# A two-layer f32 transformer kernel: the first feed-forward block in seven block products too, and modulation work cut into 1 KB slabs inside its pairs

## What is computed

```python
for l in range(DEPTH):                       # DEPTH = 2
    sh1, sc1, g1, sh2, sc2, g2, sh3, sc3, g3 = split(silu(c) @ w_mod[l] + b_mod[l], 9)
    # ... and the same nine rows from c_ctx for the context tokens
    x = x + 0.5 * g1 * swiglu(modulate(x, nw[0], sh1, sc1), ffn1_up[l], ffn1_down[l])
    # ... token mixer: w_in projection, pooling, gated linear attention, sigmoid gates, w_out
    x = x + 0.5 * g3 * swiglu(modulate(x, nw[2], sh3, sc3), ffn2_up[l], ffn2_down[l])
return rmsnorm(x, final_norm_w)
```

## Time and profile before

| what | value |
|---|---|
| median of 3 runs | 2866.95 us (2865.28 to 2867.62) |
| the profiled execution | 2867.43 us |
| its span, first to last instruction | 2865.6 us |
| instructions | 40473 |
| TensorE (PE) busy | 2824.5 us, 99% |
| PE weight loads busy | 2473.3 us, 86% |
| VectorE (DVE) busy | 1803.7 us, 63% |
| ScalarE (ACT) busy | 917.3 us, 32% |
| mean granted TensorE clock | 0.997 |
| DMA | 275.41 MB, mean 96 GB/s |

### The profile page before, as it was taken

How to read it: one execution, slowest core, us unless ns; L and a number is a source line. 1 busy time by engine, 2 the same in 40 slices (tenths; PEclk the granted TensorE clock), 3 DMA queues, 4 the chain that set the end, 5 groups by cost and what they waited for, 6 DMA issues and landing times.

```text
span 2865.6 us, 40473 instructions
## 1 busy us (share of the span) xinstructions
PE 2824.5 (99%) x15912; PEld 2473.3 (86%) x15912; DVE 1803.7 (63%) x3089; ACT 917.3 (32%) x1403; POOL 246.0 (9%) x257
## 2 busy tenths in 40 slices
PE   7999999999999999999999999999999999999998
PEld 6888888888888888899999889999988778888886
DVE  4676676657447738677766767785756667553334
ACT  4221211254332224232333523322445333432223
POOL 1000000022700011000000200000021600200000
PEclk9999999999999999999999999999999999999999
DMA  7344444322124424324122342232223144333332
GB/s 241 101 132 121 120 122 130 98 74 52 30 72 128 118 64 123 91 67 117 54 81 69 91 119 61 81 97 73 71 54 98 41 121 144 111 110 96 95 96 81
DMA packets 462077, 275.41 MB, mean 96 GB/s; under 512 B 15914, under 2 KB 460116, under 8 KB 461908
## 3 DMA queue, kind: packets, MB, share of 16 engines
q1 hardware_dynamic: 459700, 269.09, 33.0%
q10 hardware_dynamic: 2208, 4.00, 0.4%
HBM read 270.95 MB, written 2.10 MB: 95 GB/s over the span
## 4 chain that ended last, share of the span: by engine, by line
PE 93%; DVE 3%; ACT 2%; issue 1%; DMA 1%; SPq 0%; POOL 0%; ACTq 0%; POOLq 0%; DVEq 0%
PE ps L1609 44%; PE ps L1623 22%; PE ps L1862 11%; PE ps L1869 5%; PE ps L1830 2%; PE ps L1655 2%; PE ps L1835 1%; PE ps L974 1%; PE ps L954 1%; DVE wlo L2262 1%; ACT whi L1960 0%; DMA wraw<-in_ffn_up 0%; ACT hhi L2025 0%; PE ps L942 0%; DVE hlo L2366 0%
## 5 line engine op out<-in xcount | busy, mean ns | idle before, releaser
L1609 PE MATMUL ps<-hhi,whi 128*128 128x512 f32 x2112 | 625.6, 357 | 1.4 <-ACT whi L1960 1.4
L1609 PE MATMUL ps<-hlo,whi 128*128 128x512 f32 x2112 | 617.5, 353 | 0.0
L2262 DVE TENSOR_TENSOR wlo<-wraw,whi 128x1024 fp32r<-128x1024 f32 (+2 forms) x331 | 363.1, 1100 | 331.1 <-ACT whi L1960 328.7
L1960 ACT ACTIVATE whi<-wraw 128x1024 fp32r<-128x1024 f32 (+2 forms) x323 | 310.9, 963 | 721.3 <-PE ps L1623 615.2
L1623 PE MATMUL ps<-hhi,wlo 128*128 128x512 f32 x2112 | 437.2, 355 | 0.0
L1609 PEld LDWEIGHTS ps<-hhi,whi 128*128 128x128 f32 x2112 | 344.2, 189 | 61.1 <-issue 3.6
L1623 PEld LDWEIGHTS ps<-hhi,wlo 128*128 128x128 f32 x2112 | 342.4, 188 | 58.5 <-issue 3.2
L1609 PEld LDWEIGHTS ps<-hlo,whi 128*128 128x128 f32 x2112 | 343.8, 188 | 56.6 <-issue 0.5
L2281 DVE SCALAR_TENSOR_TENSOR macc<-modraw,cond,macc 128x256 f32<-128x256 f32 x588 | 240.9, 481 | 0.0
L1609 PE MATMUL ps<-mhi,whi 128*128 128x512 f32 x576 | 176.8, 359 | 0.0
L1609 PE MATMUL ps<-mlo,whi 128*128 128x512 f32 x576 | 176.1, 358 | 0.0
(11 more groups left out here) (299 smaller groups left out, 4702.5 us busy)
## 6 DMA issues: line engine op xcount, KB each, us to landing
wraw<-in_ffn_up SPq DMA_DIRECT2D x176, 512.0 KB, 4.8
modraw<-in_w_mod SPq DMA_DIRECT2D x84, 512.0 KB, 3.6
wraw<-in_w_in SPq DMA_DIRECT2D x64, 512.0 KB, 4.0
wraw<-in_ffn_down SPq DMA_DIRECT2D x64, 384.0 KB, 4.1
wraw<-in_ffn_down SPq DMA_DIRECT2D x32, 512.0 KB, 4.1
wraw<-in_w_mod SPq DMA_DIRECT2D x64, 256.0 KB, 3.1
first_mod<-in_w_mod SPq DMA_DIRECT2D x8, 1024.0 KB, 12.1
wraw<-in_w_out SPq DMA_DIRECT2D x16, 512.0 KB, 3.7
```

What stands on the lines that cost most here:

```text
L1609: nc.tensor.matmul(o, whi[:, slot, k, :], a[:, k * NT + t0:k * NT + t0 + n], start=(k == 0 and a is hi), stop=False)
L1960: nc.scalar.activation(whi[:, slot2, k, n], wraw[:, slot4, k, n], ACT.Copy).then_inc(hi_split, 1)
L2262: ins = nc.vector.tensor_tensor(wlo[:, slot2, k, n], wraw[:, slot4, k, n], whi[:, slot2, k, n].bitcast(F32), ALU.subtract)
```

## The change

Block (0,0) becomes a block with fast groups, in the four groups of the others. The modulation jobs that it hosted have to go elsewhere, and for that there is a *flow*: in every block with fast groups five jobs are cut into 40 slabs of one chunk (128 partitions of 1 KB). Fast pairs take two slabs each, one ahead of the sum at L2556 (slot 0) and one ahead of that at L2561 (slot 1); the `down` phase of the four-chunk group takes 3, 3, 3 and 0. So the slabs are 0 to 11 in the first fast group, 12 to 19 in the second, 20 to 28 in the down phase, 29 to 39 in the last, and slabs 7, 15, 23, 31 and 39 end a job with the transpose and the reduction. The ring for the loads has three places, and the transposed copy (`turned_flow`) lies over two of them. So the load of a job's first two slabs waits for the reduction of the job before. Each phase in which a flow job ends forms a batch of its own. Besides, the `down` phase that makes the token sums hosts one job, the gates loop of layer 0 one more (11), and the first group of (1,1) four instead of two. `mtmp_fast` has one buffer instead of two, `stmp_fast` half a buffer, the early silu waits for `late_m`, and the transposed copy of a job in a fast block's `down` phase lies over its second slab, whose load now waits for the reduction.

```diff
-FAST = {(0, 1): 1, (1, 0): 1}
-FFN_JOBS = {(0, 0): (6, 4, 8, 4, 6, 0), (0, 1): (6, 0, 0, 3, 0, 0, 0, 0), (1, 0): (6, 0, 0, 3, 0, 0, 0, 0),
-            (1, 1): (2, 0, 0, 0, 0, 0)}
-GATES_SPOTS = ([(i, place) for i in range(1, DC) for place in ((0, 1, 2) if i < DC - 1 else (0, 1))],
+FAST = {(0, 0): 1, (0, 1): 1, (1, 0): 1}
+FFN_JOBS = {(0, 0): (4, 1, 0, 3, 0, 0, 0, 0), (0, 1): (6, 1, 0, 3, 0, 0, 0, 0), (1, 0): (6, 1, 0, 3, 0, 0, 0, 0),
+            (1, 1): (4, 0, 0, 0, 0, 0)}
+FLOW_JOBS = 5
+RING = 3
+GATES_SPOTS = ([(0, 2), *((i, place) for i in range(1, DC) for place in (0, 1, 2))],
...
             add("up", layer, n, ffn, t, jobs[2 * t], parts=parts, lead=2 if t == 0 and (layer, ffn) in ((0, 0), (1, 1)) else 0,
-                fast=t >= FAST.get((layer, ffn), len(groups)))
+                fast=t >= FAST.get((layer, ffn), len(groups)),
+                flow=(2,) * n if t >= FAST.get((layer, ffn), len(groups)) else ())
             add("down", layer, DC // 2, ffn, t, jobs[2 * t + 1], parts=parts,
+                flow=(3, 3, 3, 0) if (layer, ffn) in FAST and n < DC // 2 + 1 else (),
...
+    turned_flow = lay("turned_flow", [P, 4 * P])
...
-    stmp_fast = lay("stmp_fast", [P, NT])
-    lay("pad_trows", [P, P])
+    stmp_fast = lay("stmp_fast", [P, HALF])
+    flow_first = lay("flow_first", [P, 2, 2 * P])
...
-    mtmp_fast = lay("mtmp_fast", [P, 2, NT])
+    mtmp_fast = lay("mtmp_fast", [P, NT])
...
-                elif ph["kind"] == "gates" and s == 1:
+                elif (ph["kind"] == "gates" or ph["kind"] == "down" and is_fast(ph)) and s == 1:
                     sp.wait_ge(mod_reduced, j)
...
+            def load_flow(ph, n):
+                for f in ph["flow"][n] if ph["flow"] else ():
+                    job, k = flow_number[f // DC], f % DC
+                    layer = (job >= MODJ) * 1
+                    if f == ph["flow"][0][0]:
+                        sp.wait_ge(mod_reduced, ph["seq"])
+                    if f >= RING:
+                        sp.wait_ge(flow_step, 2 * (f - RING + 1))
+                    if k < 2 and f >= DC:
+                        sp.wait_ge(flow_reduced, f // DC)
+                    sp.dma_start(ring_at(f), wm[layer][:, k, (job - layer * MODJ) * 2 * P:(job - layer * MODJ + 1) * 2 * P]
+                                 ).then_inc(flow_loaded[f % RING], 16)
...
+                            if isinstance(i, int):
+                                load_flow(ph, 2 * i + h)
...
                 for j in fast_pairs(ph):
                     for s in range(2):
                         load_unit(u0 + 2 * j + s, (u0 + 2 * j + s) % 4,
                                   up[:, :, s * D_FF + (f0 + j) * P:s * D_FF + (f0 + j + 1) * P], DC)
+                    load_flow(ph, j)
...
+            def flow(ph, n, which):
+                for f in [*ph["flow"][n]][which] if ph["flow"] else ():
+                    k = f % DC
+                    dve.wait_ge(flow_loaded[f % RING], 16 * (f // RING + 1))
+                    for c in range(2):
+                        if k == 0:
+                            ins = nc.vector.tensor_scalar(macc_flow[:, c, :], ring_at(f), cond[:, c * DC:c * DC + 1],
+                                                          None, ALU.mult)
+                        else:
+                            dve.wait_ge(flow_step, 2 * f - 1 + c)
+                            ins = nc.vector.scalar_tensor_tensor(
+                                out=macc_flow[:, c, :], in0=ring_at(f), scalar=cond[:, c * DC + k:c * DC + k + 1],
+                                in1=macc_flow[:, c, :], op0=ALU.mult, op1=ALU.add)
+                        ins.then_inc(flow_step, 1)
+                    if k == DC - 1:
+                        dve.wait_ge(flow_step, 2 * (f + 1))
+                        nc.vector.transpose(turned_flow[:], macc_flow[:].rearrange("p c n -> p (c n)")
+                                            ).then_inc(flow_turned, 1)
+                        dve.wait_ge(flow_turned, f // DC + 1)
+                        nc.vector.tensor_reduce(mred_flow[:, f // DC % FLOW_JOBS], turned_flow[:].rearrange("p (j n) -> p j n", n=BLK),
+                                                mybir.AxisListType.X, ALU.add).then_inc(flow_reduced, 1)
...
                         m_early(j - 1)
                         fast_lo_term(ph, j, 4)
                         m_lo(j - 1)
+                    flow(ph, j, slice(0, 1))
                     dve.wait_ge(term_done, done + 2)
                     dve.wait_ge(first_kept, q + 1)
                     steps.link(nc.vector.tensor_tensor(u2[:], fast_bank(p, 1), u2[:], ALU.add))
                     if j == 0 and jobs_pending(ph):
                         mod_finish(jobs_pending(ph))
                     fast_lo_term(ph, j, 5 if j else 4)
+                    flow(ph, j, slice(1, 2))
                     dve.wait_ge(term_done, done + 3)
                     nc.vector.tensor_tensor(late, fast_bank(p, 2), u2[:], ALU.add).then_inc(fifth_read, 1)
...
```

More of the change, by code:

```diff
@@ L104, in make_plan, with add @@
 def make_plan():
-    plan, unit, pair, job, fast_pairs = [], 0, 0, START_JOBS, 0
-    def add(kind, layer, pairs, ffn=0, third=0, jobs=0, units=None, parts=BOTH, ahead=None, fast=False, lead=0):
-        nonlocal unit, pair, job, fast_pairs
+    plan, unit, pair, job, fast_pairs, seq, flowed, numbers = [], 0, 0, START_JOBS, 0, 0, 0, []
+    def add(kind, layer, pairs, ffn=0, third=0, jobs=0, units=None, parts=BOTH, ahead=None, fast=False, lead=0, flow=()):
+        nonlocal unit, pair, job, fast_pairs, seq, flowed
+        slabs, first = [], flowed
+        for n in flow:
+            n = min(n, DC * FLOW_JOBS * ([*FAST].index((layer, ffn)) + 1) - flowed)
+            slabs.append(range(flowed, flowed + n))
+            flowed += n
+        done = range(first // DC, flowed // DC)
         units = 2 * pairs if units is None else units
         plan.append(dict(kind=kind, layer=layer, ffn=ffn, third=third, unit=unit, pair=pair, parts=parts, ahead=ahead,
-                         pairs=pairs, units=units, job=job - lead, lead=lead, jobs=jobs, fast=fast, first_fast=fast_pairs))
-        unit, pair, job = unit + units, pair + pairs, job + jobs
+                         pairs=pairs, units=units, job=job - lead, lead=lead, jobs=jobs, seq=seq, flow=slabs, done=done, fast=fast, first_fast=fast_pairs))
+        unit, pair, job, seq = unit + units, pair + pairs, job + jobs, seq + jobs
+        plan[-1]["turn"] = job
+        numbers.extend(range(job, job + len(done)))
+        job += len(done)
         fast_pairs += pairs if fast else 0
@@ L138, in make_plan @@
     assert job == DEPTH * MODJ
[L139 removed]
+    return plan, numbers
 def proj_pairs():
@@ L428, in build @@
     mod_reduced = sem("mod_reduced")
+    flow_loaded = [sem(f"flow_loaded{i}") for i in range(RING)]
+    flow_step = sem("flow_step")
+    flow_turned = sem("flow_turned")
+    flow_reduced = sem("flow_reduced")
     mod_done = sem("mod_done")
@@ L609, in jobs_of, with seq_of, ring_at @@
     def jobs_of(ph):
-        n0 = ph["job"] + ph["lead"]
-        return n0, n0 + ph["jobs"]
+        n0 = ph["job"] + ph["lead"] if ph["jobs"] else ph["turn"]
+        return n0, n0 + (ph["jobs"] or len(ph["done"]))
+    def seq_of(ph, job):
+        return job - ph["job"] - ph["lead"] + ph["seq"]
+    def ring_at(f):
+        return (flow_first[:, 0], flow_first[:, 1], flow_last[:])[f % RING]
     def halves_at(ph, i, h, place, jobs):
@@ L621, in halves_at @@
             return ((ph["job"] + q // 2, q % 2),)
+        if makes_t(ph):
+            return ((ph["job"], i),) if ph["jobs"] and h == 0 and place else ()
         hosted = 2 * i + h < ph["jobs"] if ph["kind"] == "down" and is_fast(ph) else jobs
@@ L641, in slab_count @@
         each = slabs(ph) // 2
-        return 16 * each * job + 16 * (before - each * jobs_of(ph)[0] + s // 2 + 1)
+        return 16 * each * (job - ph["job"] - ph["lead"]) + 16 * (before + s // 2 + 1)
     def mod_work(ph):
@@ L656, in mred_of @@
     def mred_of(ph):
+        if ph["kind"] == "down" and is_fast(ph):
+            return mred_down, 0
         return (mred_gates, 0) if ph["kind"] == "gates" else (mred, plan.index(ph) % 2)
     def jobs_before(ph):
-        return min(ph["job"] + ph["jobs"], DEPTH * MODJ)
+        return min(ph["turn"], DEPTH * MODJ)
     def m_base(l, ffn, third=0):
@@ L804, in jobs_pending @@
         before = plan[plan.index(ph) - 1] if ph is not plan[0] else ph
-        return before if before["jobs"] and ph is not plan[0] else None
+        return before if (before["jobs"] or before["done"]) and ph is not plan[0] else None
     def batches_before(ph):
-        return sum(1 for p in plan[:plan.index(ph)] if p["jobs"])
+        return sum(1 for p in plan[:plan.index(ph)] if p["jobs"] or p["done"])
     def peeled(ph, a):
@@ L2267, in mod_add @@
             def mod_add(ph, job, half):
-                n, per = job - START_JOBS, DC // slabs(ph)
```

(3 more changed lines are left out.)

90 lines of the change are left out of this document (58 added, 32 removed).

## The result

The changed kernel takes **2894.94 us** (median of 4 runs, 2893.39 to 2897.51) against 2867.28 for the kernel before beside it: ratio 1.0098, 95% interval 1.0086 to 1.011. It is slower by 28 us. The forecast was 2879.5 us, and the time lies 2 us above the upper end of the range, 2893. The profiled execution took 2895.91 us, its span is 2894.1.

The account below looks back on a forecast made before the run. TensorE, busy for 99% of the span, was taken as the bound, every pause in it paid in full. A gain of 36.4 us and the added costs summed to +12.5 us on 2867.43; forecast 2879.5 us, range 2855 to 2893.

Parts of the forecast that it names:

- (a): Block (0,0) in seven products instead of eight: its stretch becomes like its fellows', -36.4 us, bounds -33 and -38.
- (c): First pair of each fast group: DVE has hardly a gap, so two slabs make the critical sum late, 8.6 us.
- (e): Second pair, last fast group: weight units queue behind slab 32's load, which waits for slab 31's reduction; 14.7 us.
- (f): Four-chunk down phase: slabs 24 and 25 wait for slab 23's reduction ahead of the third pair's units; 7.2 us.
- (g): Five more batches a block, four small TensorE matmuls each, behind a phase's first unit: 0.4 us each, 6.0 us.
- (h): First group of block (1,1): four jobs for two, DVE falls behind TensorE, 1.15 us each, 2.3 us.
- (k): TensorE's clock may fall to half after the three long pauses of (e): 0 to 4.5 us, taken as 2.
- (j): Fewer buffers, and down jobs' second slab loading after the reduction, 1.4 us later but still early: 0.
- (i): Gates loop takes one more job, hidden in DVE's idle time between splits: 0, up to 3 us if cover fails.
- A: Queue not held: SP issues units before the waits, or they land in time; 2855.5 us, chance 0.15.
- C: DVE simply full: small waits make every steady pair 0.3 us longer, +10, 2889.5 us, chance 0.15.
- B: All slab work is hidden; only (a), (g) and (h) count, 2839 us, chance 0.05.

Follow-up runs that it names:

- run 2: Changed kernel with 3, 3, 2 and 0 slabs in the four-chunk down phase, so slab 31 is its pair's last: 2882.00 us, ratio 1.0059.
- run 3: Changed kernel with only SP's order altered: slabs whose load waits for their own pair's reduction go behind the next pair's weight units: 2878.22 us, ratio 1.0049.
- run 8: Two jobs moved from (1,1) to layer 1's gates loop, against the kernel with four repairs and first-pair slabs late: 2857.04 us, ratio 0.9961.
- run 9: Changed kernel, down job behind token sums, job ends late, first fast pairs without slabs, four-chunk down phase 4, 4, 4, 2: 2870.30 us, ratio 1.0015.
- run 10: As run 9, but SP issues the next pair's weight units ahead of the slabs in the four-chunk down phase: 2844.84 us, ratio 0.9919.
- run 4: Changed kernel without any work of the 120 flow slabs, a zero written for each reduction, batches kept: 2858.11 us, ratio 0.9973.
- run 5: Changed kernel with transpose and reduction of slabs 7 and 15 late in their pair, ahead of the sixth term's sum: 2883.91 us, ratio 1.0064.

## Why the prediction was wrong

By its own steps, with what each came to. The steps against the kernel before are summed over the three blocks.

| step | predicted | measured | from |
|---|---|---|---|
| (a) | -36.4 | -35.9 | stretch of (0,0): 535.1 less its own losses of 19.1, against 551.9 |
| (b) | 0 | 0.35 | steady pairs 14.69 to 14.71; one of 15.05, the third of (0,1)'s first fast group, which takes 14.69 without slab work |
| (c) | 8.6 | 7.8 | first pairs, after less no slab work: 0.68 + 0.98 + 0.95, three times |
| (d) | 8.1 | 8.0 | six pairs of 16.03 against 14.70 |
| (e) | 14.7 | 14.1 | 4.3 (19.03 less 14.70, no half clock) and 5.0 and 4.7, as the pauses there were 4.23 and 3.91 us for 3.54 |
| (f) | 7.2 | 4.6 | after less no slab work: 1.46 + 1.78 + 1.35 |
| (g) | 6.0 | 8.1 | phases without slab work less before: 0.39 + 0.93 + 0.35 + 0.38 + 0.66 a block |
| (h) | 2.3 | 3.4 | 95.55 against 92.14 |
| (k) | 2.0 | 3.7 | 21.22 and 21.59, each less 14.70, and less the 5.0 and 4.7 |
| not in the sum | 0 | 16.8 | first down phases: 5.3 + 5.3 + 6.2, half clock and all |

(a) is what remains of the stretch of (0,0) when its losses are taken off, not a measurement by itself. The rest of the kernel gave 1.3 us back, 1.0 of it in the stretch where the half clock of the earlier trace rows is gone. The ordinary group of (1,0) was 0.95 us shorter than before (84.57 us for 85.52, from the start of the stretch), for a cause that is open. That makes 28.7, where the spans differ by 28.5.

**The step that failed is (j).** It is the only step that speaks of the jobs in down phases, and it asked when the job's second slab would be loaded and gave 0 for it. The sum has no term for the job that the change puts into the first down phase of each block, and no reason for leaving it out: its place in DVE's program was not asked for. The runs show 16.8 us in its place. The diff puts one job into the phase that makes the token sums, and half of it on DVE stands between the split of a unit and t_sums; behind t_sums is ACT, and in ACT's queue, behind the rounding of those sums, is the split that TensorE needs. This is a chain through two engines that are busy for only 39.2 (DVE) and 14.5 us (ACT) of the phase's 56.5. In (e) the prediction had named what is queued behind the moved work and who waits for that; for this phase it did not ask. Run 1 shows the cause by moving the job behind the token sums: 14.9 of the 16.8 us go. With this term the sum would have been right to 1 us: 12.5 + 16.8 = 29.3 against 28.5. That closeness is luck, since the other misses nearly cancel: (g), (k) and (h) came out 2.1, 1.7 and 1.1 larger, (f), (c) and (e) 2.6, 0.8 and 0.6 smaller.

**(e)** was right in its mechanism and nearly in size: the reduction ended at T+5.4 and the units went out at T+5.9, both as said, and a sum was 3.5 to 4.2 us late for 4.9, with another 0.8 us in the pair on top. Runs 2 and 3 isolate it. **(f)** was right in mechanism (the pause of 1.75 us stands before the fifth unit, at 1447.83; run 3: 34.40 us with the units ahead) and too large. **(g)**: the batch itself costs 0.38 us, as said; two down phases are longer by 0.5 and 0.3 us besides, spread over their matmuls; why is open. **(i)** 0, as said: the stretch with the gates loop of layer 0 shows no loss. What more it could carry no run shows; the loop of layer 1 had no room for two jobs more (run 8).

**The rivals.** A fell: the queue is held (runs 2, 3, 9 and 10). C fell, since all steady pairs but one keep 14.70. B fell, since the slabs cost 36.8 us (run 4). D and E fell; (0,0) gets the pace of its fellows.

**The clock.** The prediction took 1.5 us as lost in the stretch of the earlier trace rows. Its own count of matmuls, 13 for 19 at 0.175 us, gives 1.05; the pace there, two matmuls in 0.64 us (796.36 to 797.00) for 0.35 at full clock (800.00 to 800.35), gives the 1.5. It allowed 0 to 4.5 us for three pauses and took 2; those three cost 3.7. There were three more, in the first down phases. Five of the six were followed by half clock; the part of it in the 16.8 us is about 5.4 by an estimate, since a phase with such a pause at full clock was 3.8 us longer at most (54.72 against 51.26 with a pause of 3.23 us in run 2, 55.01 with one of 3.55 in run 5).

## What to carry to other kernels

When a change puts work onto an engine that is one third idle, walk that engine's program at each place, not its busy share: who waits for the next instruction, and what is queued behind the waiter on its own engine. A load that waits for a result of its own stage belongs behind the loads of the next stage, in one queue with a fixed order; that alone was worth 15 to 17 us in run 3, and some 25 us between runs 9 and 10. And work that costs a stall in one phase may be free in another of the same block: nine or twelve slabs in a down phase cost 0, two in a first pair 0.7 to 1.0 us. Where a phase ends with preparations for the next one, work written behind them falls into the next one, as the last two slabs of run 10 did.

## What the runs showed of the hardware that was not expected

**The half clock is likely, not certain, after a pause.** In the changed kernel TensorE paused three times for 3.56 to 3.60 us in the first down phases and for 3.54, 4.23 and 3.91 in the last groups. Five pauses were followed by 3.4 to 6.8 us at 0.50; the one of 3.54 us in the last group of (0,0) was not, and in run 1 one of 3.41 us in the same place was (PEclk 0.96 above). Over the profiles of runs 2 to 5, the twelve first down phases, with pauses of 2.4 to 3.8 us, showed a mean clock of 0.94 or 0.97 eight times (55.5 to 57.9 us) and of 1.00 four times (54.0 to 55.0 us); the pauses of the two sorts overlap (2.42 us with half clock behind it, 3.55 without). The Trainium skill, "TensorE: Matmul & The Clock Gate", section "Why this matters for your kernels", says that pauses longer than about 3 us between bursts bring the half clock back; the traces agree for most such pauses and not for all. Shorter ones are not safe either: beside the one of 2.42 us, two of 1.87 and 1.86 us in the four-chunk down phases of run 9 had 3.4 us at 0.50 behind them, and a third of 1.85 us had not. A sum should take such a term with a chance. Before the change shows the half clock too, with no pause of TensorE over 0.9 us in the 96 us in front of it.

**The length of the half-clock stretch is not fixed either.** It was 3.4 us after three of the pauses and 6.8 after two, and that added about 1.5 or 2.3 us to the pause itself.
